# Rotated scores of latent attention as products of stacked high and low parts, and another order inside the dilated steps

## What is computed

```python
# first block, latent attention, 4 heads, blocks of 128 queries, causal
s = (einsum('bqhd,bkhd->bhqk', qn, k_nope)        # 128 features per head
     + einsum('bqhr,bkr->bhqk', qp, k_pe)) * scale # 64 rotated features, one k_pe for all heads
p = softmax(where(mask, s, -inf)); out = einsum('bhqk,bkhe->bqhe', p, v)

# second block, dilated window attention, 8 heads of 64, dilations 1, 4, 16
s = einsum('bdnqhe,bdnkhe->bdnhqk', qb, kw) * E ** -0.5 - slopes * dist
p = exp(s - logsumexp(s)); o = einsum('bdnhqk,bdnkhe->bdnqhe', p, vw)
```

## Time and profile before

| | |
|---|---|
| median of 3 runs | 4030.14 us |
| the others | 4026.63 and 5849.84 us |
| profiled execution | 4028.66 us |
| its span | 4026.6 us |
| PE busy | 3971.8 us of the span |
| DVE, ACT busy | 2200.1 us, 1474.6 us |

### The profile page before, as it was taken

How to read it: one execution, slowest core, us unless ns; L and a number is a source line. 1 busy time by engine, 2 the same in 40 slices (tenths; PEclk the granted TensorE clock), 3 DMA queues, 4 the chain that set the end, 5 groups by cost and what they waited for, 6 DMA issues and landing times.

```text
span 4026.6 us, 47436 instructions
## 1 busy us (share of the span) xinstructions
PE 3971.8 (99%) x18802; PEld 3072.1 (76%) x18802; DVE 2200.1 (55%) x3449; ACT 1474.6 (37%) x2422; POOL 111.8 (3%) x178
## 2 busy tenths in 40 slices
PE   9999999999999999999999999999999999999998
PEld 6787657888888878656888888777777777887786
DVE  7787667433434665566534334643546363546664
ACT  5444464211213434555312122333434343224533
POOL 2010000000000000000000000000000000000000
PEclk9999999999999999999999999999999999999999
DMA  7534101333322321201223221231111111116542
GB/s 260 198 111 141 40 11 32 101 93 109 93 96 84 90 68 56 73 1 43 63 89 91 77 68 48 73 110 43 45 41 47 42 43 63 47 57 222 188 162 79
DMA packets 99622, 342.13 MB, mean 85 GB/s; under 512 B 11016, under 2 KB 12072, under 8 KB 98250
## 3 DMA queue, kind: packets, MB, share of 16 engines
q1 hardware_dynamic: 78522, 258.87, 19.7%
q0 software_dynamic: 20880, 80.23, 6.4%
HBM read 304.45 MB, written 34.60 MB: 84 GB/s over the span
## 4 chain that ended last, share of the span: by engine, by line
PE 86%; DVE 8%; ACT 3%; issue 2%; DMA 1%; DVEq 0%; POOL 0%; ACTq 0%; POOLq 0%
PE PS L1308 35%; PE PS L1290 19%; PE PS L2407 4%; PE PS L2266 3%; PE PS L3313 2%; PE PS L3377 2%; PE PS L2176 2%; PE PS L1273 1%; PE PS L1984 1%; PE PS L2697 1%; PE PS L1703 1%; PE PS L2144 1%; PE PS L2724 1%; PE PS L2710 1%; PE PS L1990 1%
## 5 line engine op out<-in xcount | busy, mean ns | idle before, releaser
L641 ACT ACTIVATE WH<-raw 128x1024 fp32r<-128x1024 f32 x314 | 330.5, 1052 | 673.3 <-PE PS L1308 443.8
L1290 PE MATMUL PS<-hi,WH 128*128 128x512 f32 x1248 | 524.9, 421 | 0.4 <-DVE WL L652 0.2
L1308 PE MATMUL PS<-hi,WL 128*128 128x512 f32 x1312 | 515.4, 393 | 0.0
L1308 PE MATMUL PS<-lo,WH 128*128 128x512 f32 x1312 | 514.8, 392 | 0.0
L1308 PE MATMUL PS<-hi,WH 128*128 128x512 f32 x1312 | 512.5, 391 | 1.2 <-DVE WL L652 0.7
L1290 PE MATMUL PS<-hi,WL 128*128 128x512 f32 x1248 | 492.2, 394 | 0.0
L1290 PE MATMUL PS<-lo,WH 128*128 128x512 f32 x1248 | 489.1, 392 | 0.0
L652 DVE TENSOR_TENSOR WL<-raw,WH 128x1024 fp32r<-128x1024 f32 x274 | 335.0, 1223 | 122.7 <-ACT WH L641 122.6
L1308 PE MATMUL PS<-al,WH 128*128 128x512 f32 x768 | 301.5, 393 | 0.0
L1308 PE MATMUL PS<-ah,WL 128*128 128x512 f32 x768 | 301.2, 392 | 0.0
L1308 PE MATMUL PS<-ah,WH 128*128 128x512 f32 x768 | 300.1, 391 | 0.0
(11 more groups left out here) (491 smaller groups left out, 6915.6 us busy)
## 6 DMA issues: line engine op xcount, KB each, us to landing
adab<-in_w_ada POOLq DMA_DIRECT2D x120, 512.0 KB, 4.6
raw<-in_win SPq DMA_DIRECT2D x104, 512.0 KB, 3.6
raw<-in_down SPq DMA_DIRECT2D x80, 512.0 KB, 3.6
raw<-in_up SPq DMA_DIRECT2D x64, 512.0 KB, 3.6
raw<-in_dft SPq DMA_DIRECT2D x24, 512.0 KB, 3.9
sp_x<-X SPq DMA_DIRECT2D x24, 512.0 KB, 6.2
X<-sp_x SPq DMA_DIRECT2D x24, 512.0 KB, 5.1
raw<-in_wout SPq DMA_DIRECT2D x24, 512.0 KB, 3.7
```

The costliest lines, as they stand in the source:

```text
L641: act.activation(PLACES[PLACE[j]][0], raw[:, j % 2, :], ACT.Copy).then_inc(*W_HI.next(j))
L1290: mm = pe.matmul(bank[b + hf], w[:, k, :], r[:, k, HALF[hf]], start=k == 0 and w is wh and r is hi, stop=k == 7 and w is wl)
L1308: mm = pe.matmul(bank[b + hf], w[:, k, :], r[:, k, HALF[hf]], start=k == 0 and w is wh and r is hi, stop=k == 7 and w is wl)
```

## The change

Rotated scores: the rotated keys are split into a high part `khigh` (ACT copy to float32r) and a low part `klow` (DVE, what is left), each written to both partition halves. The rotated queries of each head get a tile `qs[h]` of their own whose one half is the high part and whose other half the low part. A block's rotated scores are now products over all 128 rows in float32r: `khigh` with the stacked queries (high x high plus high x low), then `klow` with the same. In columns of up to 512 these are 4 matmuls for a large block and 2 for a small one. Three of the four `qs` tiles lie in `wol`, which is free there. `LONG` gets new entries, so some units behind them move in the order.

```diff
-                qx0 = sb(c, "qx0", [P, S])
+                self.klow = sb(c, "klow", [P, S], R)
-                self.kp = sb(c, "kp", [P, S])
+                self.khigh = sb(c, "khigh", [P, S], R)
-                self.qx = [qx0, sb(c, "qx1", [P, S])]
+                self.qs = [sb(c, "qs0", [P, S], R), self.wol[1][:, 2, :], self.wol[0][:, 0, :], self.wol[0][:, 1, :]]
...
-        LONG = {"norm": 5.0, "newton": 7.5, "project": 2.5, "rotate": 3.5, "copy": 1.0, "exchange": 0.9, "values": 3.0}
+        LONG = {"norm": 5.0, "newton": 7.5, "project": 2.5, "rotate": 3.5, "split keys": 2.0, "split queries": 1.8, "values": 3.0}
...
+        ROWS = (slice(0, 64), slice(64, P))
+        def split_queries(u):
+            return [(m.qs[u.head + x], ROWS[x], ROWS[1 - x]) for x in range(2)]
...
+                elif u.kind == "split keys":
+                    act.wait_ge(*unit_done(l, u.after))
+                    for to in ROWS:
+                        act.activation(m.khigh[to, HALF[u.hf]], m.misc[R64, HALF[u.hf]], ACT.Copy).then_inc(
+                            *ML_ACT.next("high", l, lane, u.i, to.start))
+                elif u.kind == "split queries":
+                    act.wait_ge(*unit_done(l, u.after))
...
+                    for to, own, other in split_queries(u):
+                        act.activation(to[own, HALF[u.hf]], u.src[own, HALF[u.hf]], ACT.Copy).then_inc(
+                            *ML_ACT.next("high", l, lane, u.i, own.start))
...
-                elif u.kind == "exchange":
-                    yield u.at
+                elif u.kind == "split queries":
+                    yield u.at + 1
                     dve.wait_ge(*unit_done(l, u.after))
-                    dve.tensor_copy(u.dst[64:128, HALF[u.hf]], u.src[0:64, HALF[u.hf]])
-                    dve.tensor_copy(u.dst[0:64, HALF[u.hf]], u.src[64:128, HALF[u.hf]]).then_inc(
-                        *ML_DVE.next("done", l, lane, u.i))
+                    for to, own, other in split_queries(u):
+                        dve.wait_ge(*ML_ACT["high", l, lane, u.i, own.start])
+                        step = dve.tensor_tensor(to[other, HALF[u.hf]], u.src[own, HALF[u.hf]],
+                                                 to[own, HALF[u.hf]].bitcast(F), ALU.subtract)
+                    step.then_inc(*ML_DVE.next("done", l, lane, u.i))
...
-            mm = pe.matmul(s[:, 0:min(HS, w)], m.qp[hp, h // 2, qb * P:(qb + 1) * P], m.kp[hp, 0:min(HS, w)], start=False,
-                           stop=True)
-            if large:
-                mm = pe.matmul(s[:, HS:w], m.qx[h // 2][other, qb * P:(qb + 1) * P], m.kp[other, HS:w], start=False,
-                               stop=True)
+            for keys in (m.khigh, m.klow):
+                for k0 in range(0, w, HS):
+                    n = min(HS, w - k0)
+                    mm = pe.matmul(s[:, k0:k0 + n], m.qs[h][:, qb * P:(qb + 1) * P], keys[:, k0:k0 + n], start=False,
+                                   stop=keys is m.klow)
```

```diff
         def dilated_pe(pe):
             for s in range(BLOCKS + 2):
                 yield block_at(s)
+                if 1 <= s <= BLOCKS:
...
+                    pe.wait_ge(*DA_ACT["exp", s - 1])
+                    if s == 1 or s % 8 == 0 and s < BLOCKS:
+                        pe.wait_ge(*DA_ACT["values", s // 8, value_groups(s // 8)[-1][0]])
+                    if s > 1:
+                        pe.wait_ge(*DA_DVE["turned", s - 2])
+                    for x in range(2 * blocks):
+                        mm = pe.transpose(PS[:, 6, x * P:(x + 1) * P],
+                                          SC[:, b % 2, x // blocks, x % blocks * P:(x % blocks + 1) * P], ident[:, :])
+                    mm.then_inc(*DA_PE.next("turned", s - 1))
                 if s < BLOCKS:
```

More of the change, by code:

```diff
@@ L1901, in rotary @@
                 u = put(lane, "rotate", hf, when[2], src=m.qp[:, i, :], dst=m.qp[:, i, :], rows=P, after=u)
-                return put(lane, "exchange", hf, src=m.qp[:, i, :], dst=m.qx[i], after=u)
+                return put(lane, "split queries", hf, src=m.qp[:, i, :], head=2 * i, after=u)
             heads, tq, tkv, tkp = {}, [], [], []
@@ L1919, in mla_units @@
             for hf in range(2):
-                u = put(2 * hf + 1, "rotate", hf, src=m.misc, dst=m.kp[:, :], rows=64, after=tkp[hf])
-                heads["turned", 0] += [rotary(2 * hf, 0, hf), put(2 * hf + 1, "copy", hf, after=u)]
+                u = put(2 * hf + 1, "rotate", hf, src=m.misc, dst=m.misc, rows=64, after=tkp[hf])
+                heads["turned", 0] += [rotary(2 * hf, 0, hf), put(2 * hf + 1, "split keys", hf, after=u)]
             heads["v", 0] = [put(2 * hf + 1, "values", hf, head=0, after=tkv[hf]) for hf in range(2)]
@@ L1974, in mla_pe @@
                 yield u.at + (1 if u.kind in ("norm", "newton") else 0)
-                if u.kind in ("copy", "exchange"):
+                if u.kind in SPLITS:
                     continue
                 if u.i:
-                    pe.wait_ge(*bank_left(l, units[u.i - 1 - (units[u.i - 1].kind in ("copy", "exchange"))]))
+                    pe.wait_ge(*bank_left(l, units[u.i - 1 - (units[u.i - 1].kind in SPLITS)]))
                 else:
@@ L2006, in head_left @@
                 e.wait_ge(*AT_PE["out", l, h - 2, 3])
+        SPLITS = ("split keys", "split queries")
+        ROWS = (slice(0, 64), slice(64, P))
+        def split_queries(u):
+            return [(m.qs[u.head + x], ROWS[x], ROWS[1 - x]) for x in range(2)]
         def mla_act(act, l, lane):
@@ L2012, in mla_act @@
             for u in units:
-                yield u.at + (0 if u.kind in ("norm", "newton") else 0.6 if u.kind == "values" and (u.head, u.hf) == (1, 0) else 1.8)
+                yield u.at + (0 if u.kind in ("norm", "newton", *SPLITS) else 0.6 if u.kind == "values" and (u.head, u.hf) == (1, 0) else 1.8)
                 if u.kind in ("norm", "newton"):
@@ L2121, in attend_pe @@
             at, z, w, large = pair_of(l, h, qb), h % 2, (qb + 1) * P, qb > 3
-            hp, other = (slice(64 * x, 64 * x + 64) for x in (h % 2, 1 - h % 2))
             lanes, heads = mla_units(l)
@@ L2675, in dilated_pe @@
                 yield block_at(s)
+                if 1 <= s <= BLOCKS:
+                    u, b = divmod(s - 1, 8)
+                    w = width_of(u)
+                    blocks = w // P
+                    pe.wait_ge(*DA_ACT["exp", s - 1])
[7 more added lines that the diff above has]
+                    mm.then_inc(*DA_PE.next("turned", s - 1))
                 if s < BLOCKS:
@@ L2699, in dilated_pe @@
                     mm.then_inc(*DA_PE.next("scores", s))
[L2700 to L2707, removed]
-                        pe.wait_ge(*DA_DVE["turned", s - 2])
-                    for x in range(2 * blocks):
-                        mm = pe.transpose(PS[:, 6, x * P:(x + 1) * P],
-                                          SC[:, b % 2, x // blocks, x % blocks * P:(x % blocks + 1) * P], ident[:, :])
-                    mm.then_inc(*DA_PE.next("turned", s - 1))
                 if s >= 2:
```

15 lines of the change are left out of this document (11 added, 4 removed).

## The result

The changed kernel took 4007.8 us (median of four; 4006.6 to 4008.0), the kernel before 4026.0, 4026.6 and 4030.1 us on the same chip: a ratio of 0.995, 95% interval 0.9931 to 0.997. A fourth execution of the kernel before, of 5849.8 us, is left out, since it was in a slower state. On the mean that is 20 us less. The time lies inside the range, and the gain is about half of the 42 that the forecast of 3988 asked for. So the sign and the place were right and the size was off.

The account below looks back on a forecast made before the run. PE's instruction stream was taken as the bound nearly everywhere. 4028.7 (profiled execution) - 15.2 (dilated steps) - 26.7 (rotated scores, 33.9 less 7.2 of waits) = 3986.8, or 3988 us on the median's scale; range 3974 to 4012.

Parts of the forecast that it names:

- Dilated steps: Dilated attention: transposes moved ahead of scores leave three changes of shape instead of four, 0.16 us per step, 15.2 us saved.
- the pair without a row: Dilated step: scores straight to values, a transition in no profile row, taken to cost like the other changes of shape.
- the moved wait: Dilated step: moved transposes wait for the previous block's exponential; cover at the tightest step falls from 1.1 to 0.6 us.
- Rotated products on PE: Latent attention: full-row float32r products cut a head from 8.56 to 4.32 us, 33.9 us over 8 heads.
- the third rival: Narrow float32r matmuls run at the plain float32 price, 5 us from attention before waits, 4010 us; chance 0.06.
- What of it becomes a wait: Latent attention: savings lost at PE's waits for norm squares and scaled probabilities, 3.6 us per layer, 7.2 in all.
- The ring: Attention's cycle PE, DVE, ACT, DVE, PE, in which a faster PE could meet DVE and ACT.
- The first rival: Attention chains take more of the gain: only 10 of the 33.9 us stay, 4005 us; chance 0.17.
- The splits: Key and query splits add 7.6 us on ACT and 4.0 on DVE per layer; priced zero, without cover 1 to 2.
- The first-head part: Ahead of head 0: 4 us of cover by the output projection's gemm against 2 us more for two query units.
- The gemm stretches: Gemms elsewhere in the program: the prediction called itself wrong if these changed.
- The slower rival: Dilated step: row split straight to column split makes the array run empty; at 0.6 us per step 4045 us; chance 0.03.

Follow-up runs that it names:

- one to three passes: Changed kernel with the low-part key products left out (one pass, 3999.3 us) or added twice (three passes, 4013.2 us); two passes is the changed kernel itself.
- run again: The changed kernel unaltered, measured once more beside the follow-up versions: 4005.7 us.
- the dilated part alone: Kernel before with only the dilated steps' transposes put ahead of the scores, attention as before: 4019.3 us.
- split earlier: Changed kernel with one query split per layer (head 2, first half) further ahead in ACT's and DVE's queues: 4004.2 us.
- both: Changed kernel with DVE's copy of the turned block ahead of the softmax work and the head 2 query split earlier: 3999.6 us.
- all three: Changed kernel with turned-block copy first, head 2 query split earlier, and large blocks' transposes one piece earlier in 7 of 16 blocks per layer: 3993.6 us.

## Why the prediction was off by half

**Dilated steps, 15.2 forecast, 9.1 measured.** The price of 0.16 us a step was right to the hundredth, and so was the pair without a row. (The steps with all three pieces are 94 and not 95, which is 0.2 us.) What failed is the sentence "Behind the moved wait stand the scores, values and the next gemm; none of them is delayed while 0.6 is left." It follows one consumer, the exponential. The scores came 0.53 later in the step, and with them everything that DVE does on them, and behind that in DVE's queue stood a copy that had nothing to do with the scores. The next unit's value transposes waited for it. Shown: with the copy ahead of the scores' work the waits went and 6 us came back.

**Rotated products on PE, 33.9 forecast.** This held. The group shown above takes 0.8 to 0.9 us, changes of shape are gone, and the third rival is ruled out. With the narrow products at the prices of the last section instead of mine it would be about 35, an estimate. In each layer all that stands behind attention came 6.4 us earlier relative to what stands ahead of it, of 17.0 taken out of each.

**"What of it becomes a wait", 3.6 a layer forecast, about 10.6 measured.** This is the step that failed most. I counted the waits that the trace already had, and took their places to be the only tight ones. The ring behind them had slack that I didn't work out, and the term for the waits came out at a third of its size. Each block's value products need copies of 0.6 to 0.7 us that run under the rotated products, and the next scores need an exponential. When the cover shrank by 0.3 to 0.8 us, the slack was used up at most blocks. From start to start, the value products of a layer come 6.7 us later in sum than behind finished copies, 1.2 before, so 5.5 is new; the exponential's waits add 2.4, the normed query's 1.2, the norm's squares 0.5. That is 9.6 of 10.6; the last 1.0 I can't place. The dose of PE's work (one to three passes) shows that the cover is what counts; that the copies and the exponential are the whole of the chain is read from the waits, since no run took these waits away. The first rival said this (4005, "only 10 of the 33.9 stay"); 12.7 stayed, and I had given it 0.17. My argument against it, "most blocks of heads 0 to 2 do not wait", was true of a PE that was slower.

**The splits, priced zero, 1.8 a layer measured.** This is no further loss but a part of the 10.6: the waits of head 1 are counted there. The first-head part was right: all of ACT's and DVE's new work ahead of the first scores cost nothing. For head 2 I said that there was a whole head of time. There was for the result, but the split also holds up what stands behind it in two queues, and that was the 1.13 and 1.19 at 521.65 and 524.40.

**The gemm stretches** elsewhere did not change, but for a fall of the clock at 1450.6 us in the profile of the kernel before, which cost 1.6 us there and is in no other profile. The slower rival did not come.

## What to carry to other kernels

Where one engine is 98% busy, taking work out of its stream is worth the full amount only up to the slack of what that work covered: for each shortened piece, find the copies on other engines that run under it and who reads them, and compare their end with the new start. When a piece is moved in one engine's order, follow the queues of its consumers too, and ask what unrelated instruction stands behind them. Here the repairs were only orders of instructions: a copy put ahead of work that it did not depend on, a split put earlier, and transposes put ahead of another product. Together they gave back 12.6 us.

## What the runs showed of the hardware

Behind the two waits of head 1 the granted clock sometimes fell for a little over 3 us, from the 2.4 GHz level to the 1.2 GHz level. The windows of the kernel after, run again, where it did, and of its first profile, where it did not. Head 1 comes 2 us later in the first profile, so the windows stand 2 us later too:

```profile
521.00:525.00 4.00, 2.81 (x6) 1.15 (x6) 2.57 (x8) 1.83 (x5) 0.00 (x0) 0.69 0.00 0
525.00:529.00 4.00, 4.00 (x10) 1.84 (x9) 2.65 (x7) 2.06 (x4) 0.00 (x0) 0.88 0.00 0
```

```profile
523.00:527.00 4.00, 2.81 (x9) 1.31 (x8) 3.31 (x9) 1.83 (x5) 0.00 (x0) 1.00 0.00 0
527.00:531.00 4.00, 4.00 (x16) 2.20 (x15) 3.11 (x7) 3.07 (x6) 0.00 (x0) 1.00 0.00 0
```

In both PE had been idle for 1.1 us and, after about 1.6 us of work, for another 1.2. Where the clock fell, a record of 512 plain float32 columns behind them took 1.06 us instead of 0.59, and the stretch 1.5 to 1.7 us more. It happened in 5 of the 16 layers of the eight versions with that pair of waits, in none of the 10 layers of the five without it (before, the dilated part alone, split earlier, both, all three). But a pair is not needed. In the gemm stretch at 1450 us of the kernel before the clock fell behind a single wait of 1.0 us, timeline of PE and window:

```profile
1448.15 2.00 PE L1703 MATMUL PS<-X 64*128 64x64 f32 x32 [1.00 <-DVE X L1614]
1450.00:1454.00 4.00, 4.00 (x14) 3.09 (x13) 3.17 (x6) 0.41 (x1) 0.00 (x0) 0.57 0.00 0
```

It also fell in two of the five versions without the pair (split earlier, both), at about 1545 us, behind a single wait of 0.8. So in some executions a wait of about 1 us costs 1.5 us more than its length. Which waits do that, and that they are the cause, no run here shows.

Float32r matmuls of fewer than 512 columns cost in proportion: from start to start 0.23 for 512 columns, 0.17 for 384, 0.12 for 256 and 0.06 for 128, the last below the 0.11 that I had taken for a floor.
